# Where the experts' bias products stand in their accumulation, and what the reads of g, u and y wait for

## The reference

```
gu  = ragged_dot(x_sorted, w_up, group_sizes) + b_up[e_sorted]      # 1024 -> 2048
g   = min(gu[:, :1024], 7);  u = clip(gu[:, 1024:], -7, 7)
act = (u + 1) * (g * sigmoid(1.702 * g))
out = ragged_dot(act, w_down, group_sizes) + b_down[e_sorted]       # 1024 -> 1024
y   = segment_sum(out * gate weight, token)
```

## Time and profile before

| | us |
|---|---|
| median of 3 runs | 2371.75 (2371.46 to 2371.77) |
| the profiled execution, its own time | 2371.01 |
| its span (first to last instruction) | 2369.3 |
| PE busy | 2126.9 (90%) |
| VectorE busy | 1649.7 (70%) |
| ScalarE busy | 1248.5 (53%) |
| share of PE at L1621 in the chain that ended last | 66% |

### The profile page before, as it was taken

The page is one execution under the profiler, slowest core; times in us unless marked ns, Lnnn a source line. Parts: engine busy times, 40 slices in busy tenths (PEclk is TensorE's granted clock), DMA queues, the critical chain, the costliest instruction groups (busy, mean ns, idle before and its releaser), DMA issues.

```text
span 2369.3 us, 30053 instructions
## 1 busy us (share of the span) xinstructions
PE 2126.9 (90%) x9452; PEld 1634.0 (69%) x9452; DVE 1649.7 (70%) x1797; ACT 1248.5 (53%) x1419; POOL 202.5 (9%) x141
## 2 busy tenths in 40 slices
PE   4999799879769999955999999999999999999967
PEld 3777677768645555434877878778778787787746
DVE  4676756668451111135999999999999999999955
ACT  3444243332310010013787777777877777787744
POOL 0000000101000000021021110111101111110020
PEclk9999899989879999967999999999999999999989
DMA  3225222112023222065999999999999999999672
GB/s 97 77 55 195 55 80 63 51 38 71 18 92 104 78 55 62 29 231 181 356 364 389 367 369 382 366 385 374 359 387 370 370 383 366 384 370 365 242 244 87
DMA packets 244019, 527.68 MB, mean 223 GB/s; under 512 B 19830, under 2 KB 127942, under 8 KB 243974
## 3 DMA queue, kind: packets, MB, share of 16 engines
q1 hardware_dynamic: 228688, 481.73, 56.4%
q0 software_dynamic: 7424, 25.19, 3.0%
q10 hardware_dynamic: 7862, 20.19, 2.1%
HBM read 497.55 MB, written 29.49 MB: 222 GB/s over the span
## 4 chain that ended last, share of the span: by engine, by line
PE 70%; DVE 14%; issue 8%; ACT 4%; DMA 2%; ACTq 0%; SPq 0%; DVEq 0%; POOL 0%; POOLq 0%
PE psum L1621 66%; DVE h_lo L1491 4%; ACT h_hi L941 1%; DVE w_lo L1486 1%; PE psum L1901 1%; DVE arena L1506 1%; DVE arena L1189 1%; DVE arena L1509 1%; DVE arena L1516 1%; DVE residual L1564 1%; PE psum L1788 1%; PE psum L1741 1%; DMA arena<-in_final_norm_w 1%; PE psum L1628 1%; DMA arena<-in_lambda_k 0%
## 5 line engine op out<-in xcount | busy, mean ns | idle before, releaser
L1491 DVE TENSOR_TENSOR h_lo<-arena,h_hi 128x1024 fp32r<-128x1024 f32 x768 | 912.0, 1222 | 90.8 <-ACT h_hi L941 54.2
L941 ACT ACTIVATE h_hi<-arena 128x1024 fp32r<-128x1024 f32 x768 | 801.0, 1059 | 219.4 <-PE psum L1621 200.2
L1621 PE MATMUL psum<-h_hi,w_hi 128*128 128x512 f32 x2176 | 870.1, 400 | 20.2 <-DVE h_lo L1491 12.9
L1621 PE MATMUL psum<-h_hi,w_lo 128*128 128x512 f32 x2176 | 850.2, 391 | 0.0
L1621 PE MATMUL psum<-h_lo,w_hi 128*128 128x512 f32 x2176 | 850.2, 391 | 0.0
L1621 PEld LDWEIGHTS psum<-h_hi,w_hi 128*128 128x128 f32 x2176 | 410.9, 189 | 124.7 <-DVE h_lo L1491 26.0
L1621 PEld LDWEIGHTS psum<-h_hi,w_lo 128*128 128x128 f32 x2176 | 410.1, 188 | 87.4
L1621 PEld LDWEIGHTS psum<-h_lo,w_hi 128*128 128x128 f32 x2176 | 411.0, 189 | 84.9 <-issue 3.8
L1621 PE MATMUL psum<-arena 128*128 128x512 f32 (+7 forms) x1232 | 358.3, 459 | 39.5 <-DVE arena L1383 13.4
L1621 PEld LDWEIGHTS psum<-arena 128*128 128x128 f32 (+1 forms) x1232 | 188.4, 198 | 196.4 <-issue 153.8
L1055 DVE TENSOR_TENSOR w_lo<-arena,w_hi 128x1024 fp32r<-128x1024 f32 x80 | 100.5, 1257 | 131.1 <-ACT w_hi L744 130.9
(11 more groups left out here) (264 smaller groups left out, 1547.3 us busy)
## 6 DMA issues: line engine op xcount, KB each, us to landing
arena<-in_w_up SPq DMA_DIRECT2D x512, 512.0 KB, 7.3
arena<-in_w_down SPq DMA_DIRECT2D x256, 512.0 KB, 6.3
arena<-in_w_in SPq DMA_DIRECT2D x80, 512.0 KB, 3.9
y_dram<-arena ACTq DMA_DIRECT2D x32, 512.0 KB, 8.4
arena<-in_w_ssd_branch SPq DMA_DIRECT2D x8, 1024.0 KB, 5.6
y_dram<-arena SPq DMA_DIRECT2D x1, 7680.0 KB, 23.1
arena<-in_w_attn_branch SPq DMA_DIRECT2D x8, 512.0 KB, 3.7
arena<-in_w_out SPq DMA_DIRECT2D x2, 2048.0 KB, 13.3
```

Of the source, the lines that this page charges most:

```text
L941: act.activation(piece_hi[slot], rows, ACT.Copy).then_inc(piece_hi_ready, 1)
L1491: dve.tensor_tensor(piece_lo[slot], rows, piece_hi[slot].bitcast(F32), ALU.subtract).then_inc(piece_lo_ready, 1)
L1621: return pe.matmul(o, l, r, start=start, stop=stop)
```

## The change

The four bias products of `up` and the two of `down` come first in their accumulations and carry its start flag; the last product of the last piece carries the stop flag. The semaphores raised after them are renamed `bias_up_added` and `bias_dn_added` and now say only that the bias has been read. The readers of the results wait for the piece that completes their banks instead: g for up piece 14, u for up piece 15, y for down piece 7.

```diff
@@ SP
             def load_bias_up(i, expert):
-                wait(sp, up_done, i)
+                wait(sp, bias_up_added, i)
             def load_bias_down(i, expert):
-                wait(sp, down_done, i)
+                wait(sp, bias_dn_added, i)
@@ ScalarE
             def expert_out(b):
-                act.wait_ge(down_done, b + 1)
+                act.wait_ge(piece_used, down_piece(b, DOWN_PIECES - 1) + 1)
@@ VectorE
             def take_g(b):
-                dve.wait_ge(up_done, b + 1)
+                dve.wait_ge(piece_used, up_piece(b, UP_PIECES - 2) + 1)
                 dve.tensor_scalar(g_sb, psum[:, 0:FF], LIMIT, None, ALU.min).then_inc(g_ready, 1)
             def take_u(b):
+                dve.wait_ge(piece_used, up_piece(b, UP_PIECES - 1) + 1)
                 dve.tensor_scalar(u_sb, psum[:, FF:2 * FF], LIMIT, -LIMIT, ALU.min, ALU.max).then_inc(u_ready, 1)
@@ PE
             def piece(slot, k, l_hi, l_lo, b):
                 for n in range(2):
                     ins = mm3(bank(b + n), l_hi[:, k, :], l_lo[:, k, :], piece_hi[slot][:, n, :],
-                              piece_lo[slot][:, n, :], k == 0, False)
+                              piece_lo[slot][:, n, :], False, k == KT - 1)
                 ins.then_inc(piece_used, 1)
             def up(b):
                 pe.wait_ge(x_lo_ready, b + 1)
                 wait(pe, u_ready, b)
+                pe.wait_ge(bias_up_landed, 16 * (b + 1))
+                for n in range(4):
+                    ins = mm(bank(n), ones_bf[:], bias_up[:, n * 512:(n + 1) * 512], True, False)
+                ins.then_inc(bias_up_added, 1)
                 for i in range(UP_PIECES):
                     wait_up_lo(pe, b, i)
                     piece(i % 4, i // 2, x_hi, x_lo, 2 * (i % 2))
-                pe.wait_ge(bias_up_landed, 16 * (b + 1))
-                for n in range(4):
-                    ins = mm(bank(n), ones_bf[:], bias_up[:, n * 512:(n + 1) * 512], False, True)
-                ins.then_inc(up_done, 1)
             def down(i):
                 pe.wait_ge(actt_ready, i + 1)
                 wait(pe, y_ready, i)
+                pe.wait_ge(bias_dn_landed, 16 * (i + 1))
+                for n in range(2):
+                    ins = mm(bank(4 + n), ones_bf[:], bias_dn[:, n * 512:(n + 1) * 512], True, False)
+                ins.then_inc(bias_dn_added, 1)
                 for k in range(KT):
                     wait_down_lo(pe, i, k)
                     piece(k % 4, k, act_hi, act_lo, 4)
-                pe.wait_ge(bias_dn_landed, 16 * (i + 1))
-                for n in range(2):
-                    ins = mm(bank(4 + n), ones_bf[:], bias_dn[:, n * 512:(n + 1) * 512], False, True)
-                ins.then_inc(down_done, 1)
```

More of the change, by code:

```diff
@@ L399, in build @@
         bias_cleared, gather_cleared = sem("bias_cleared"), sem("gather_cleared")
-        (block_token_ready, xg_landed, x_turned, up_done, g_ready, u_ready, sig_ready,
-         act_ready, act_turned, actt_ready, act_hi_ready, x_hi_ready, x_lo_ready, down_done, y_ready, y_stored, bias_up_landed,
+        (block_token_ready, xg_landed, x_turned, bias_up_added, g_ready, u_ready, sig_ready,
+         act_ready, act_turned, actt_ready, act_hi_ready, x_hi_ready, x_lo_ready, bias_dn_added, y_ready, y_stored, bias_up_landed,
          bias_dn_landed) = (sem(n) for n in (
-            "block_token_ready", "xg_landed", "x_turned", "up_done",
+            "block_token_ready", "xg_landed", "x_turned", "bias_up_added",
             "g_ready", "u_ready", "sig_ready", "act_ready", "act_turned", "actt_ready",
-            "act_hi_ready", "x_hi_ready", "x_lo_ready", "down_done", "y_ready", "y_stored", "bias_up_landed", "bias_dn_landed"))
+            "act_hi_ready", "x_hi_ready", "x_lo_ready", "bias_dn_added", "y_ready", "y_stored", "bias_up_landed", "bias_dn_landed"))
         piece_hi_ready, piece_used = sem("piece_hi_ready"), sem("piece_used")
```

## The result

| | before | after |
|---|---|---|
| median, us | 2371.75 | 2383.80 |
| lowest and highest of 5 | 2370.35 to 2372.48 | 2380.16 to 2385.87 |
| profiled execution, its own time | 2371.01 | 2383.80 |
| its span | 2369.3 | 2382.0 |

After stands to before as 1.0050 (95% interval 1.0039 to 1.0062): slower by 12 us, where 10 were forecast.

What follows compares the result with a forecast made beforehand. PE was taken to set the pace except before down piece 6, where VectorE's chain decides. Start 0.9, rounds 11.1 and end -2.0 sum to 10.0 us slower, a median of 2381.8 us; range 2373.0 to 2387.5.

Steps and rivals of the forecast that it cites:

- The place of the cost: Each round, 0.43 us of PE work moves from the covered stretch before down piece 6 to the uncovered one after it.
- T: Moment PE finishes the last up piece; VectorE's chain from there to PE's start of down piece 6 stays 10.33 us.
- SP's release: SP's queue no longer waits at two bias loads; later loads leave up to 3 us earlier, gaining 0 per round.
- The bias of the next up product: Now needed at that product's front; 16.3 us of cover against piece loads of 7.3 median, 15.7 longest; cost 0.
- where the stall grows: PE's wait before down piece 6 grows by starts from 0.58 to about 1.01 us a round.
- the weight load: At a piece's first matmul after transposes, 0.08 us extra should vanish behind bias products; 0.06 us a round taken off.
- the end: After the last block, the bias and gate weights leave 2.0 us earlier: -2.0 us, bounds -2.0 and +1.5.
- the start: In blocks 0 and 1, the bias products of up(1) run with nothing beside them: +0.9 us.
- A: PE, not VectorE's chain, sets the whole round; faster, 2365.8 us; chance 0.07.
- B: No measurable change, as part of PE's stall returns or weight loads hide more; centre 2373.5 us; chance 0.13.
- C: PE's clock falls behind the longer stop each round, 60 us more, about 2442 us; chance 0.02.
- D: The next up product's bias lands late and PE waits before up, 15 us more, 2397 us; chance 0.05.

Runs made afterwards that it cites:

- g1: Full change, with VectorE's join behind the remainders of down 5, 6 and 7 and take_g ahead of the remainder of down 2: 2347.63 us, 0.990 of before.
- g2: Full change, with join behind the remainders of down 5, 6 and 7 and take_u behind the remainder of down 5: 2349.86 us, 0.9907 of before.
- e4: Full change, with VectorE's take_g ahead of the remainder of down 2 instead of behind that of down 3: 2370.55 us, 0.9994 of before.
- f4: Full change, with SP's bias loads held until the last up and down pieces are through, as before: 2382.96 us, 1.0045 of before.
- e3: Full change, with VectorE's join behind the remainder of down 6 instead of ahead of it: 2377.54 us, 1.0027 of before.
- f1: Full change, with VectorE's join behind the remainders of down 5, 6 and 7: 2356.02 us, 0.9931 of before.
- f2: Kernel before, changed only by moving join behind the remainders of down 5, 6 and 7: 2349.31 us, 0.9902 of before.
- e1: Full change with the down bias put back last, so only the up bias stands first: 2398.92 us, 1.012 of before.
- e2: Full change with the up bias put back last, so only the down bias stands first: 2364.41 us, 0.9972 of before.

## Why the prediction was right, point by point

**Right, and shown.** The place of the cost: 10.32 us from T to down 6 and 26.60 us from there to the next T. Moving one half of the products alone gives +27 and -7 us, which no theory of waits or of PE's total work gives. The move of 0.43 us a round came out as 0.425 over 30 rounds, and its price was lifted whole by removing the stalls (g1, g2: 35.74 and 35.80 us a round, and 35.77 without the change). The new waits of VectorE cost nothing, and take_g gained nothing until it was moved (e4). SP's release cost and gained nothing in the round (f4). The bias of the next up product was not late: PE waits for no load between 1140 and 2200 us. The prediction's longest landing, 15.7 us against 16.3 us of cover, was not of this stretch, where up pieces landed within 9.6 us before and 9.1 us after (18.3 over the whole execution), so there was more to spare than it said.

**Wrong in a sign: where the stall grows.** The prediction let the stall at down 6 grow by all of the 0.43 us, from 0.42 to about 0.85 us in PE's records and from 0.58 to 1.01 us by starts. It grew to 0.60 and 0.75. Some 0.2 us of the earlier arrival were lost one piece sooner, in the new stall at down 5. Both lie between T and piece 6, so the sum is right all the same; but the prediction had looked for VectorE at one piece only, and that cost the expectation of e3 its aim, and that of the difference between f1 and f2 (1 to 2 us expected, 6.7 measured).

**Wrong in size: the weight load.** I took 0.06 us a round off, since the first matmul behind transposes takes 0.08 us more than usual. The lines above show no saving. From the start of the transposes to the second matmul of the piece it is 1530.68 - 1528.71 = 1.97 us; before it was 1.10 us (0.79 and 0.31, by the earlier trace rows); the difference is 0.87 us, and four bias products were 0.88. The gap between the first two fp32r matmuls has even grown, to 0.42 us. That is 1.8 us of the 12.

**Wrong in size: the end.** I took -2.0 us; it was -0.6. The bias and all behind it did leave 2.1 us earlier after the last T (10.65 and 12.72 us behind it). But from that DMA's issue to the first gate weights SP took 4.18 us before and 5.79 us now, so these left only 0.5 us earlier (16.44 and 16.90 us behind T). Between the two SP only loads a register, branches, and passes waits long fulfilled. In f4, with the bias issued late again, it is 4.18 us as before. What makes this time vary stays open, but the runs sort it: it is 4.18 to 4.35 us in the four kernels in which SP has to stand and wait before this bias load (before, e1, f2, f4), and 4.62 to 5.79 us in the seven others that load this bias last, where it goes straight through. That the queue drains as it was filled is borne out: final_norm_w left 25.34 us behind T before and 25.75 now, yet it landed 39.27 and 38.73 us behind T, 0.5 us earlier, like the gate weights ahead of it.

**Wrong in size: the start.** +0.9 was forecast and +0.5 measured, from one execution each. Behind the stop of 4.81 us in block 1 the granted clock was 0.50 (1.2 GHz) in both kernels, and the bias products of up(1) now run in that stretch: its second fp32r matmul starts at 1124.16 and not at 1122.62, 1.5 us later and not 0.9. But PE's starts are back at 0.24 us apart from 1125.00 on, and before only from 1125.88 on, so seven slow starts of the pieces have become two, and 1.0 us comes back.

Together that is 12.74 + 0.53 - 0.57 = 12.7 us for the spans, against 11.1 + 0.9 - 2.0 = 10.0. The first two errors add up, 1.6 and 1.4 us, and the third takes 0.4 back.

**The rivals.** A fell as to the full change, but its mechanism is real one step away: in e2 PE's progress after T does set VectorE's chain, through the slot of down piece 4. B fell: the way from T to piece 6 is as long as before, and 12 us are clear of the noise. C fell: the clock stayed at 1.00 with the longer stop, 0.60 us a round in PE's records. The Trainium skill, "TensorE: Matmul & The Clock Gate", section "A second HAM failure mode: psum-queue depth-cycling", says that micro-idles between groups can make the clock swing; no stop of this length did so here. D did not occur.

## What to carry to other kernels

Work of an engine that is 99% busy is not all of one price: find where it stalls, which other engine's chain is fixed from which moment to that stall, and count a moved instruction only outside that stretch. Taking an instruction off such a chain gains only until the next piece in line becomes the late one; in e3 it was the piece behind, in f1 the piece ahead, where PE had already waited unseen; so work out the arrival of every piece around the one you free. And a change that allows an earlier read gains nothing until the reader is moved in its own engine's order: here e4 brought the change from +12 us back to the time before. The 24 us that g1 gains are nearly all the moved join's, which the kernel before can have alone (f2, 23 us).

## What the runs showed that I had not expected

A bf16 bias product between transposes and fp32r pieces hides no weight load time: the first two fp32r matmuls start 0.42 us apart behind it, 0.31 us behind transposes, and 0.227 us in the stream.

In f1 PE's matmuls list no idle time at all, and still 0.22 us a round was lost to a wait that shows only in the records of the weight load. The full change has the same wait, beside the one that its matmuls do list, and in the list of waits only the count at the weight load (58 and not 29) gives it away.
